# The first layer's shift and scale summed on TensorE in column strips instead of on VectorE

## What is computed

```python
c_act = jax.nn.silu(c)                       # c: 1 x 2048
for l in range(2):
    mod = c_act @ w_ada[l] + b_ada[l]        # w_ada[l]: 2048 x 6144
    shift, scale, gate = jnp.split(mod, 3, axis=-1)
    h = _layernorm(x) * (1.0 + scale[:, None, :]) + shift[:, None, :]
    p = h @ w_in[l]
    ...
```

## Time and profile before

| | |
|---|---|
| median of 3 runs | 1762.41 us (1757.44 to 1766.17) |
| the profiled execution | 1763.5 us |
| its span, first to last instruction | 1761.7 us |
| busy over the span | PE 88%, DVE 66%, ACT 40%, POOL 3% |
| mean granted TensorE clock | 0.96 |

### The profile page before, as it was taken

One profiled execution on the slowest core, in us unless ns is written; L12 is line 12 of the kernel. 1 busy time (PEld: TensorE's weight loads), 2 busy tenths in 40 slices (PEclk: granted clock), 3 DMA queues, 4 the chain that ended last, 5 costly groups with the idle time before them and its releaser, 6 DMA issues.

```text
span 1761.7 us, 24901 instructions
## 1 busy us (share of the span) xinstructions
PE 1545.4 (88%) x9679; PEld 1360.2 (77%) x9679; DVE 1164.1 (66%) x1961; ACT 701.4 (40%) x1193; POOL 58.1 (3%) x86
## 2 busy tenths in 40 slices
PE   1677889888993999999994999999999699999998
PEld 1667776787773988699883998888988598998886
DVE  7887746678888663557666544687565656669653
ACT  1222313333332432343433434356454435556642
POOL 3000000000000000000000000000000700000000
PEclk9978999999996999999997999999999899999999
DMA  8787676799774575467655464434555464443463
GB/s 312 270 309 266 221 217 204 271 328 323 262 274 144 186 223 141 144 218 260 202 192 163 138 185 133 132 108 121 178 181 167 123 187 138 130 146 117 140 218 112
DMA packets 184070, 342.93 MB, mean 195 GB/s; under 512 B 28972, under 2 KB 47632, under 8 KB 183184
## 3 DMA queue, kind: packets, MB, share of 16 engines
q1 hardware_dynamic: 179920, 326.88, 57.8%
q0 software_dynamic: 4032, 14.46, 2.4%
HBM read 339.14 MB, written 2.15 MB: 194 GB/s over the span
## 4 chain that ended last, share of the span: by engine, by line
PE 67%; DVE 15%; DMA 9%; ACT 5%; issue 4%; SPq 0%; DVEq 0%; POOLq 0%; POOL 0%; ACTq 0%
PE PM L1233 56%; PE PB L1233 8%; DMA stg<-in_w_in 6%; DVE wlo L1770 3%; DVE AC L1698 3%; ACT whi L1500 2%; DVE X L1698 1%; DMA stg<-in_w_ada 1%; DVE AR L1698 1%; ACT AR L1500 1%; PE PB L1360 1%; DVE SM L1967 1%; ACT TMP L1500 1%; DVE SM L1698 1%; PE PB L1403 1%
## 5 line engine op out<-in xcount | busy, mean ns | idle before, releaser
L1770 DVE TENSOR_TENSOR wlo<-stg,whi 128x1024 fp32r<-128x1024 f32 (+3 forms) x424 | 500.3, 1187 | 366.4 <-ACT whi L1500 364.0
L1500 ACT ACTIVATE whi<-stg 128x1024 fp32r<-128x1024 f32 (+3 forms) x424 | 430.8, 1023 | 529.2 <-PE PM L1233 290.8
L1233 PE MATMUL PM<-Hh,whi 128*128 128x256 f32 x1824 | 534.7, 293 | 33.8 <-DVE wlo L1770 21.3
L1233 PE MATMUL PM<-Hl,whi 128*128 128x256 f32 x1824 | 522.1, 286 | 0.0
L1233 PE MATMUL PM<-Hh,wlo 128*128 128x256 f32 x1824 | 521.8, 286 | 0.0
L1233 PEld LDWEIGHTS PM<-Hh,whi 128*128 128x128 f32 x1824 | 355.2, 195 | 48.3 <-DVE wlo L1770 24.8
L1233 PEld LDWEIGHTS PM<-Hl,whi 128*128 128x128 f32 x1824 | 355.7, 195 | 0.3
L1233 PEld LDWEIGHTS PM<-Hh,wlo 128*128 128x128 f32 x1824 | 355.3, 195 | 0.0
L1233 PE MATMUL PM<-whi,Hh 128*128 128x512 f32 (+1 forms) x704 | 279.4, 397 | 16.4 <-DVE wlo L1770 10.2
L1233 PE MATMUL PM<-wlo,Hh 128*128 128x512 f32 (+1 forms) x704 | 274.1, 389 | 0.0
L1233 PE MATMUL PM<-whi,Hl 128*128 128x512 f32 (+1 forms) x704 | 273.9, 389 | 0.0
(11 more groups left out here) (227 smaller groups left out, 1242.1 us busy)
## 6 DMA issues: line engine op xcount, KB each, us to landing
stg<-in_w_ada SPq DMA_DIRECT2D x192, 512.0 KB, 5.3
stg<-in_w_in SPq DMA_DIRECT2D x112, 512.0 KB, 5.1
stg<-in_even_w_in SPq DMA_DIRECT2D x80, 512.0 KB, 3.6
stg<-in_w_out SPq DMA_DIRECT2D x64, 512.0 KB, 5.4
stg<-in_odd_w_in SPq DMA_DIRECT2D x64, 512.0 KB, 3.6
stg<-in_even_w_out SPq DMA_DIRECT2D x32, 512.0 KB, 4.0
stg<-in_odd_w_out SPq DMA_DIRECT2D x32, 512.0 KB, 4.6
stg<-in_w_in SPq DMA_DIRECT2D x16, 320.0 KB, 4.0
```

The source lines that it names most:

```text
L1233: return e.matmul(out, l, r, start=start, stop=stop, skip_group_check=True)
L1500: return e.activation(out, x, f, **k)
L1770: e.tensor_tensor(wlo[s["lo"]][:, :, 0:n], stg[s["slot"]][:, :, 0:n], whi[s["hi"]][:, :, 0:n].bitcast(F32), ALU.subtract).then_inc(SEM["lo ...
```

## The change

Shift and scale of layer 0 are no longer accumulated on VectorE. A new kind of job, "pe", loads the same tiles, now in turns one of shift and one of scale. When a pair has landed, TensorE runs four fp32 matmuls on it (step "adap"): the stationary operand is `CZ[:, k, :]`, 32 columns of which the first holds slice k of `c` and the rest are zero; the moving operand is the staged tile's slice of 128x512; the results go to four strips of 32 partitions of one PSUM bank (shift even, shift odd, scale even, scale odd slices at partitions 0, 32, 64, 96), which collect over the eight pairs. Then ScalarE copies the bank to `AC` ("adap_out"), four matmuls against the two columns of `BLK` bring sums of shift and scale into one column per 128 values ("adap_col"), and three VectorE instructions write `MOD`. One of the two small PSUM banks is held meanwhile. Each adap step is emitted with the second job of its pair, three jobs behind the load, and only there are the two staging buffers put back in the list. `setup` hangs on job 14 instead of 12. Layer 0's gate and all of layer 1 stay as they were.

```diff
-                if j["mode"] != "ada":
+                if j["mode"] in ("split", "raw"):
...
+    def ada_pe(self, g):
+        st, out = {}, []
+        for q in range(KT // 2):
+            for half in range(2):
+                def body(job, q=q, half=half):
+                    if half == 0:
+                        st["shift"] = job
+                        if q == 0:
+                            st["bank"], st["free"] = self.now(self.banks)
+                        return
+                    other = st["shift"]
+                    mm = self.tick("adap_mm")
+                    self.step("adap", q=q, bank=st["bank"], free=st["free"] if q == 0 else (),
+                              slots=[other["slot"], job["slot"]], ld=[other["ld"], job["ld"]])
+                    self.stgs.put(other["slot"], mm)
+                    self.stgs.put(job["slot"], mm)
...
+                src = (0, 512, "w_ada0", 2 * q, half * D + g * 512)
...
-            more = self.ada(0, q * 512, 512) + self.ada(0, D + q * 512, 512) if q < 4 else []
+            more = self.ada_pe(q) if q < 4 else []
...
-        self.jobs[12]["pre"] = setup
+        self.jobs[14]["pre"] = setup
...
+        CZ = RX[:, 0:512].rearrange("p (k n) -> p k n", k=16)
...
+                elif kind == "adap":
+                    q.wait_all(s["free"])
+                    q.wait_ge(("cz", 1))
+                    for half in range(2):
+                        q.wait_ge(s["ld"][half])
+                    for i in range(2):
+                        k = 2 * s["q"] + i
+                        for half in range(2):
+                            o = 64 * half + 32 * i
+                            ins = mm(B[o:o + 32, :], CZ[:, k, :], stg[s["slots"][half]][:, i, :], s["q"] == 0, s["q"] == KT // 2 - 1)
+                    ins.then_inc(SEM["adap_mm"], 1)
...
+                elif kind == "adap_out":
+                    q.wait_ge(s["mm"])
+                    q.wait_all(s["free"])
+                    act(acc_of(dict(a=s["a"], n=512), 0), B[:, :]).then_inc(SEM["adap_out"], 1)
```

More of the change, by code:

```diff
@@ L272, in ada, with fin @@
             out.append(dict(mode="ada", src=[src], n=n, dve=body, post=fin if q == KT // per - 1 else None))
+        return out
+    def ada_pe(self, g):
[14 more added lines that the diff above has]
+                    self.stgs.put(job["slot"], mm)
+                    st["mm"] = mm
+                def fin():
+                    a, afree = self.accs.get()
+                    ev = self.tick("adap_out")
+                    self.step("adap_out", bank=st["bank"], mm=st["mm"], a=a, free=afree)
+                    self.banks.put(st["bank"], ev)
+                    b, fr = self.now(self.banks)
+                    mm, u = self.tick("ada_mm"), self.tick("mod")
+                    self.step("adap_col", bank=b, free=fr, a=a, ev=ev, mm=mm, f=4 * g)
+                    self.banks.put(b, u)
+                    self.accs.put(a, mm)
+                    self.mod[0, g] = self.mod[0, 4 + g] = u
+                src = (0, 512, "w_ada0", 2 * q, half * D + g * 512)
+                out.append(dict(mode="pe", src=[src], n=512, mm=body, post=fin if q == KT // 2 - 1 and half else None))
         return out
@@ L1032, in build @@
         names += ["x_landed", "c_landed", "const_landed", "brw_landed", "rows_landed", "pos_landed", "rel_landed",
-                  "scr_landed", "out_landed", "c_mm", "c_tanh", "c_act", "ca", "set_mm", "rope_arg", "rope_tab",
+                  "scr_landed", "out_landed", "c_mm", "c_tanh", "c_act", "ca", "cz", "set_mm", "rope_arg", "rope_tab",
                   "bias_mm", "ve", "ae"]
@@ L1285, in tensor @@
                     ins.then_inc(SEM["mm"], 1)
+                elif kind == "adap":
[9 more added lines that the diff above has]
+                    ins.then_inc(SEM["adap_mm"], 1)
+                elif kind == "adap_col":
+                    q.wait_all(s["free"])
+                    q.wait_ge(s["ev"])
+                    q.wait_ge(const)
+                    x = acc_of(dict(a=s["a"], n=512), 0)
+                    for j in range(4):
+                        ins = mm(B[:, 2 * j:2 * j + 2], x[:, j * 128:(j + 1) * 128], BLK, j == 0, True)
+                    ins.then_inc(SEM["ada_mm"], 1)
                 elif kind == "ada_col":
@@ L1715, in rsqrt @@
                 return a
+            z = seen(e.memset(CZ[:, :, :], 0.0))
             q.wait_ge(("c_tanh", 1))
@@ L1720, in vector @@
             e.tensor_scalar(CA[:, :], CA[:, :], 0.5, None, ALU.mult).then_inc(SEM["ca"], 1)
+            q.wait_ge(z)
+            q.wait_ge(("ca", 1))
+            e.tensor_copy(CZ[:, :, 0], CA[:, :]).then_inc(SEM["cz"], 1)
             def setup(s):
@@ L1783, in vector @@
                         ins.then_inc(SEM["ada"], 1)
+                elif kind == "adap_col":
+                    f = s["f"]
+                    q.wait_ge(s["mm"])
+                    q.wait_ge(("bias", 1))
+                    e.tensor_tensor(MOD[:, f:f + 4], B[:, 0:8:2], BCL[:, f:f + 4], ALU.add)
+                    dst = MOD[:, 16 + f:20 + f]
+                    a = seen(e.tensor_tensor(dst, B[:, 1:8:2], BCL[:, 16 + f:20 + f], ALU.add))
+                    q.wait_ge(a)
+                    e.tensor_scalar(dst, dst, 1.0, None, ALU.add).then_inc(SEM["mod"], 1)
                 elif kind == "ada_col":
```

## The result

The changed kernel takes 1831.36 us in the median of 4 runs (1824.32 to 1835.98); the kernel before took 1762.31 beside it. The ratio is 1.0389, 95% interval 1.0366 to 1.0413: slower, by 69 us where +61.4 to 1825 was predicted. The profiled execution took 1830.68 us with a span of 1828.9.

What follows compares the result with a forecast made beforehand. The prediction took loads and VectorE to set about 36 us a period up to block 3, TensorE the rest. Periods +63.6, start -1.4 and end -0.8 gave +61.4 on 1763.5, about 1825 us; 8 in 10 range 1802 to 1856.

Steps and rivals of the forecast that it cites:

- What bounds the kernel: Up to block 3 loads and VectorE together set about 36 us a period; from 164 us on TensorE sets the pace.
- What is removed: In the periods, 32 multiply-adds leave VectorE, 21.9 of its 30 us, worth only what the loads make of it.
- What is added: On TensorE, four strip matmuls a pair, side by side: 0.9 us at the upper level, 1.7 at the lower, plus 0.2.
- What is moved: In the periods, loads halt because buffers come back late: 56.9 us a period instead of 35.7, 63.6 over three.
- The hand schedule: One period worked out load by load from W0's landing, with the next W0 landing at 56.9 us.
- the restart after a halt: In the periods, the first load after a halt lands 3.7 us after issue, the next ones 1.33 apart.
- slow restart: In the periods, restarts slower than one load alone shows: +1.4 us for each of six, 25 more, 1850 us.
- the start: Ahead of block 0, the first jobs no longer wait behind x's layernorm: 1.4 us gained, block 0 at 55.5.
- The end term: At the end of the stage, block 3's first matmul comes at 12.9 instead of 13.7 us: 0.8 less.
- Strips in sequence: Rival on TensorE: strips run one after another, +5.3 us a period, 16 in all, 1841 us; chance 0.12.
- Hidden halts, faster: Rival in the periods: loads in flight hide the halts and the DMA engines set the pace, 1741 us; chance 0.06.
- No change: Rival in the periods: only the halts at a0 and a8 count, 2.5 us a period, 1770 us; chance 0.05.

Runs made afterwards that it cites:

- ring7_before: The kernel before, sums on VectorE, with a circle of seven staging buffers in the first stage instead of five; 1752.9 us, ratio 0.9932.
- ring11_before: The kernel before, sums on VectorE, with a circle of eleven staging buffers in the first stage instead of five; 1749.8 us, ratio 0.9907.
- one_strip: The changed kernel with all four matmuls of a pair in one strip of 32 partitions; 1849.6 us, ratio 1.0466 to the kernel before.
- late_back: The kernel before, sums on VectorE, with layer 0's w_ada buffers put back in pairs three jobs behind the load; 1817.9 us, ratio 1.0292.
- list11: The changed kernel, job order and first-in-first-out list untouched, with eleven buffers in the first stage instead of five; 1750.2 us, ratio 0.9903 to the kernel before.
- pairs_whole: The changed kernel with its pe jobs placed so that no w_in job cuts a pair; 1817.6 us, ratio 1.0295 to the kernel before.

## Why the prediction was right

**What bounds the kernel.** Right in the main: the stage's loads set its length, and what lies behind block 3 kept its length (-2.7 us). One reading was too strong. I took 36 us a period as the pace that loads and VectorE set together; ring7_before and ring11_before show 31.6 and 30.5 with the same engines, so about 4 to 5 of the 36 were the kernel before's own shortage of buffers. The 7 us between a period and its 28.6 us of loads were the place to ask; the prediction put them down to the loads and VectorE together.

**What is removed.** Right: worth nothing by itself. VectorE went from 30 to 10 busy us a period and the period got longer. Even with eleven buffers the period without the multiply-adds (31.2) isn't shorter than the one with them (30.5), and block 3 starts within 0.9 us of it (147.1 and 148.0).

**What is added.** Right: four strips at once, 1.9 us a pair at the lower clock level (1.94 in the row above), 1.07 at the upper, of which 0.9 by the distance of the starts; the forecast was 1.7 and 0.9, plus 0.2 for switching over. The estimate of 1.1 to 1.4 us that the prediction worked out from three strips is not far off at its lower end. one_strip shows the alternative.

**What is moved.** The mechanism is shown from both sides, by late_back (the buffers' order alone, +15.5 a period) and by list11 (the change with enough buffers, 33.1). The hand schedule holds step for step; in the period from 102.9 to 161.3 us, counted from W0's landing (predicted, measured): a0 lands at 6.1, 6.8; W1 8.8, 9.5; a4 14.9, 15.6; W2 24.4, 23.8; a6 30.0, 30.3; a8 37.9, 38.5; W4 40.6, 41.8; a12 46.7, 48.2; a14 54.2, 55.9; next W0 56.9, 58.4.

**The size.** +67.2 in the span against +61.4 worked out. The sum came closer than its terms did. Up to block 3 it is +69.9 where the terms gave +61.4, 8.5 too little, and 2.7 of that came back behind block 3, where the prediction had nothing; that part is luck, as the span behind block 3 differs by 11 us among the kernels of the table. Two terms hold most of the miss, and a small third is the end. First the restart after a halt, for which I took the 3.7 us of a load alone. That was right for a4 (3.7), which leaves alone, but a0, a6, a8, a12 and a14 leave with others right behind them and took 4.0 to 4.6. The issues of SyncE at 105.2 (a0) and 137.4 (a8) in the changed kernel (size, us to landing):

```profile
stg<-in_w_ada SPq DMA_DIRECT2D x1, 512.0 KB, 4.5
...
stg<-in_w_ada SPq DMA_DIRECT2D x1, 512.0 KB, 4.0
```

This is the "slow restart" that the prediction kept as a bound at +1.4 each; it was 0.3 to 0.9. The five together are 2.6 us, and W2, which landed 0.6 earlier than worked out, gives some of it back; that makes the 1.5 us by which this period was longer than 56.9 (the first was longer by 1.9). Second the start: +1.4 where I had -1.4, so that block 0, at 58.3, missed the 55 to 57 us that the prediction gave as a sign. A pair was to be replaced 1.9+3.7 us after it lands; but the pair's second load lands some 1.3 later than its first, and the strips wait for both. W0 landed at 39.7 instead of 36.5, and all behind it kept its predicted distances (the copy to VEC 3.1 late, block 0 2.8 late). Part of it is spread: pairs_whole, whose program is the same up to there, had block 0 at 56.0, its eleven loads landing 4.2 us after their issue in the middle where the changed kernel's took 5.3. The clock isn't the difference: in both, all but one of the pairs that the strips sum there take 1.6 to 1.9 us. Why the loads differ from one execution to another stays open. The end term, -0.8, did not come: block 3 started 14.6 us after its W0 landed and block 1 14.3.

**The rule and the row.** The restart that was priced from the row at 2.4 us of start-up measured 2.4 to 3.3 here for loads of 512 KB (3.7 to 4.6 less 1.33). So the trace's figure was nearer than the 2.0 of the Trainium skill (DMA: Bandwidth & Descriptors, Anatomy of one DMA), which is a fit for loads that GpSimd issues; these are issued by SyncE. Only the first part of W2, 320 KB, came close to it: 2.9 us less 0.8.

**The rivals.** Strips in sequence: excluded by the records and by one_strip, which also shows that its price was split wrongly: 3.1 us a period, not 5.3, but another 5.3 in the start, where the prediction had the pairs cost nothing. Hidden halts, faster: not in this kernel; but its condition was the right one to name, since list11, in which the halts are mostly hidden, is 1.0% faster than the kernel before. The rival's price was too good: it said 1741 with 28.6 us a period, and 1750 and 33.1 were measured. No change: excluded, W2 did wait for the pair.

## What to carry to other kernels

Where a queue issues loads in order and buffers come back through a list, moving work off a busy engine is not the change; the change is when the buffers are put back. Write down for each load which earlier tile's buffer it takes and how many loads lie between: in the second period of the changed kernel nothing landed for 5.8 to 6.8 us with no load between, for 4.0 to 5.1 with one and for 3.5 to 3.7 with two, where a full queue lands a load every 1.3 us. Before taking work off an engine, try whether more buffers alone give the time: here they gave 0.7 to 0.9% to the kernel before, and they turned the change from 4% slower into 1% faster, though no faster than the sums left where they were.

## What the runs showed of the hardware

- Four fp32 matmuls of 32 columns by 512 in four column strips of one bank took about the time of one: four records start within 0.02 us, and the next four 0.45 later. The trace of the kernel before had only shown two halves side by side.
- In the periods the granted clock was lower where TensorE stood idle for long. Over the same 188 matmul records, the changed kernel's periods had a granted clock of 0.71 to 0.74 (busy for 35 to 36 of 58 to 59 us, above), list11 0.93 in the first window below. That the loads halt isn't enough for it: in one_strip they halt as long, but TensorE is busy for 49 of 62 us, and the granted clock was 0.91 (second window).

```profile
87.00:119.00 32.00, 28.31 (x188) 19.50 (x188) 9.51 (x13) 8.26 (x11) 0.00 (x0) 0.93 0.94 336
...
125.00:187.00 62.00, 49.31 (x188) 24.97 (x188) 9.37 (x14) 8.52 (x11) 0.00 (x0) 0.91 0.55 182
```

- A granted clock of 1.00 can mean that nothing was recorded. The start of list11 has it in the view of windows:

```profile
0.00:54.00 54.00, 22.70 (x87) 6.30 (x87) 19.70 (x54) 8.99 (x11) 14.99 (x32) 1.00 0.95 336
```

The pairs there take as long as they do at the lower level, though; the timeline of pairs_whole, whose start shows 1.00 as well, has for example

```profile
24.05 1.94 PE L1271 MATMUL PB<-stg,RX 128*32 128x512 f32 x8 [0.55 <-DMA stg<-in_w_ada]
```

The first clock record of list11's trace stands at 57.5 us, that of pairs_whole at 60.0, that of the kernel before at 63.1, and a stretch without one is shown as 1.00. So the 1.00 of the kernel before's start says nothing of the level there, and the mean of 0.73 in the changed kernel's start, whose records begin at 19.3 us, can't be set against it.

- Loads of two programs that are the same up to there took 4.2 us in the middle in one execution and 5.3 in the other, and the start of block 0 differed by 2.3 us.
